# One maximum and one factor operation per attention job: a VectorE reduction over two PSUM banks

## What is computed

```python
# q, k: (B, S, DA_HEADS, 2, 64)   v: (B, S, DA_HEADS, 128)
s = jnp.einsum('bqhcd,bkhcd->bhcqk', q_blk, k).astype(jnp.float32) * scale
...
p = jax.nn.softmax(jnp.where(causal, s, -jnp.inf), axis=-1)
attn = p[:, :, 0] - lam_full * p[:, :, 1]
return jnp.einsum('bhqk,bkhe->bqhe', attn.astype(v.dtype), v)
...
o = o * lax.rsqrt(jnp.mean(o * o, -1, keepdims=True) + RMS_EPS) * subln_g * (1.0 - lambda_init)
```

## Time and profile before

| | us |
|---|---|
| median of 3 runs | 2817.95 |
| lowest and highest | 2817.34 to 2820.68 |
| the profiled execution | 2818.15 |
| its span in the trace | 2815.5 |
| second attention in it | about 959 to 1058 |

### The profile page before, as it was taken

How to read it: one execution, slowest core, us unless ns; L and a number is a source line. 1 busy time by engine, 2 the same in 40 slices (tenths; PEclk the granted TensorE clock), 3 DMA queues, 4 the chain that set the end, 5 groups by cost and what they waited for, 6 DMA issues and landing times. The chain is left out here.

```text
span 2815.5 us, 88317 instructions
## 1 busy us (share of the span) xinstructions
PE 2367.7 (84%) x38648; PEld 1634.8 (58%) x38649; DVE 1051.7 (37%) x2786; ACT 568.3 (20%) x1201; POOL 147.4 (5%) x256
## 2 busy tenths in 40 slices
PE   8987897999889989799867659978887879788982
PEld 3436655777644565577645524458886347566761
DVE  0205634333330283433212145026666643232324
ACT  1113411111230261111100021024341111011111
POOL 0000010000000011000000010011112100000001
PEclk9998999999989999899988879989998799999996
DMA  6120307898442101979999942100001349999995
GB/s 240 64 86 5 135 17 265 354 397 327 167 162 98 60 1 56 401 311 393 428 429 428 428 174 93 60 1 3 3 3 42 121 186 417 429 428 428 404 428 228
DMA packets 83114, 612.46 MB, mean 218 GB/s; under 512 B 19810, under 2 KB 40546, under 8 KB 49188
## 3 DMA queue, kind: packets, MB, share of 16 engines
q1 hardware_dynamic: 44864, 569.05, 48.8%
q10 hardware_dynamic: 31396, 20.06, 2.3%
q0 software_dynamic: 6720, 21.40, 2.3%
HBM read 578.99 MB, written 31.46 MB: 217 GB/s over the span
## 5 line engine op out<-in xcount | busy, mean ns | idle before, releaser
L1175 PE MATMUL ps<-ring,arena 128*32 128x128 f32 x13184 | 408.1, 283 | 102.6 <-DMA ring<-in_experts 72.6
L1175 PEld LDWEIGHTS ps<-ring,arena 128*32 128x32 f32 x13184 | 378.7, 114 | 144.2 <-DMA ring<-in_experts 68.8
L1152 PE MATMUL ps<-x_tok,arena 128*32 128x256 f32 x4768 | 300.5, 392 | 24.5 <-DVE arena L1289 19.7
L1382 DVE TENSOR_TENSOR arena<-arena,ps 128x64 f32<-128x64 f32 x292 | 64.8, 222 | 611.2 <-ACT arena L1234 611.2
L1234 ACT ACTIVATE arena<-ps 128x64 f32<-128x64 f32 x292 | 65.5, 224 | 1089.0 <-PE ps L1175 1089.0
L1152 PEld LDWEIGHTS ps<-x_tok,arena 128*32 128x32 f32 x4768 | 163.2, 114 | 106.2 <-issue 37.9
L1175 PE MATMUL ps<-arena 128*32 128x128 f32 x5504 | 172.9, 285 | 48.5 <-DMA arena<-in_experts 39.9
L1185 PE MATMUL ps<-ring,arena 128*32 128x256 f32 x3296 | 198.7, 379 | 9.4 <-DMA ring<-in_experts 9.4
L1175 PEld LDWEIGHTS ps<-arena 128*32 128x32 f32 x5504 | 159.6, 114 | 67.2 <-DMA arena<-in_experts 45.6
L1126 PE MATMUL ps<-ring,arena 128*128 128x512 f32 x384 | 170.7, 600 | 3.1 <-PEq L192 2.1
L1185 PEld LDWEIGHTS ps<-ring,arena 128*32 128x32 f32 x3296 | 110.2, 110 | 80.0 <-DMA ring<-in_experts 15.2
(11 more groups left out here) (418 smaller groups left out, 3068.5 us busy)
## 6 DMA issues: line engine op xcount, KB each, us to landing
ring<-in_experts SPq DMA_DIRECT2D x165, 2048.0 KB, 21.5
arena<-in_experts SPq DMA_DIRECT2D x50, 2048.0 KB, 24.7
xt_mem<-in_experts SPq DMA_DIRECT2D x25, 2048.0 KB, 29.2
ring<-in_mixer_chunks SPq DMA_DIRECT2D x24, 2048.0 KB, 12.4
xybuf<-arena ACTq DMA_DIRECT2D x608, 32.0 KB, 6.7
xybuf<-arena SPq DMA_DIRECT2D x1, 9216.0 KB, 25.6
rows<-in_ln_g POOLq DMA_DIRECT2D x6, 512.0 KB, 7.4
rows<-in_ln_b POOLq DMA_DIRECT2D x6, 512.0 KB, 8.4
```

Source lines behind the costliest of these rows:

```text
L1152: ins = pe.matmul(ps[to, 5, 0:W], one_hot[:, j, :], x_tok[:, j, q * W:(q + 1) * W], start=(j == 0), stop=(j == NT - 1))
L1175: ins = pe.matmul(ps[at, 2 + half, 0:P], xg[:, k, :], w_gu[half][:, k, q, :], start=(k == 0), stop=(k == NK - 1))
L1382: dve.tensor_tensor(hidden[:, half, :], silu_g[:, half, :], ps[:, 2 + half, HALF:P], ALU.mult)\
```

## The change

For `n_comp == 2` the two maxima of a job are taken by one TENSOR_REDUCE whose input is both banks (128 partitions x 2 x width) and whose output is two columns, and both factors by one TENSOR_SCALAR on two columns. DVE waits once, for both score tiles. The semaphore `dve_a` is counted up once per job instead of twice, and both of ACT's exponentials wait for that one count. The first attention (`n_comp == 1`) takes the same path as before.

```diff
-            m0, x0, e0 = pe_a.take(jobs * n_comp), dve_a.take(jobs * n_comp), act_a.take(jobs * n_comp)
+            m0, x0, e0 = pe_a.take(jobs * n_comp), dve_a.take(jobs), act_a.take(jobs * n_comp)
...
                             for c in range(n_comp):
-                                act.wait_ge(dve_a.sem, x0 + n_comp * s + c + 1)
+                                act.wait_ge(dve_a.sem, x0 + s + 1)
...
+                    def joint_maxima(n):
+                        m = st[:, n % DEEP, :]
+                        dve.wait_ge(pe_a.sem, m0 + 2 * n + 2)
+                        link(dve.tensor_reduce(m[:, 0:2], ps[:, 2 * (n % 2):2 * (n % 2) + 2, 0:width(n)], AX, ALU.max))
+                        dve.tensor_scalar(m[:, 2:4], m[:, 0:2], -SCALE, None, ALU.mult).then_inc(dve_a.sem, 1)
+
                     def maxima(n):
                         m = st[:, n % DEEP, :]
+                        if n_comp == 2:
+                            return joint_maxima(n)
                         for c in range(n_comp):
```

## The result

| | before | after |
|---|---|---|
| median of 20 runs, us | 2819.27 | 2826.46 |
| lowest and highest | 2814.76 to 2824.20 | 2822.44 to 2833.59 |
| profiled execution (its span) | 2818.15 (2815.5) | 2828.93 (2827.2) |
| second attention, first product to last head | 99.04 | 107.29 |
| DVE busy in it | 78.60 | 72.43 |

The ratio is 1.0026, with a 95% interval of 1.0019 to 1.0032. That is 7.2 us more, where +2.2 was forecast, and 2826.46 lies above the range (2825.0). The middle of the interval is over the bound of 0.2%, its lower end just under it; to "slower by over 0.2%" 0.18 had been given. The kernel before was measured 1.3 us above the three runs that the forecast started from; that leaves 5.0 us between the forecast difference and the measured one.

A forecast was written before the change was run, and what follows sets the result against it. A loop of dependences, no engine full, bounds the steady head. Five heads' 2.2, first interval's 0.17 and -0.15 for table load and tail give +2.2 us: 2820.2 us after taking off 0.20, range 2816.0 to 2825.0.

The forecast's parts named there:

- A: Steady head, 512-wide maximum's start to the 256-wide job's product on PE: 3.16 us, forecast +0.32 through ACT's queue.
- Rival 3: Joint reduction over two banks is dear: +1.06 us a head, 2826.6 us in all; chance 0.07.
- rival 1: DVE's whole saving arrives: 8.0 us less, 2810.0 us; chance 0.05.
- the last addend of A: Step from the end of ACT's store to PE's product, taken as 0.05 us from a PE weight load.
- B: Steady head, from the 384-wide job's maxima to the next waiting product on PE: 2.63 us, forecast +0.12.
- PE's stretches: The two parts of a steady head where PE works without pause, 1.80 and 2.67 us, forecast unchanged.
- The head: One steady head of the second attention, 10.26 us between 512-wide maxima, forecast +0.44 in five intervals.
- First interval: Interval from job 3's maxima, with no store to wait for: forecast +0.17 us or so.
- table load: Job 27's head, exponentials behind a table load: up to 0.25 us gained; -0.15 taken with the stage's end.
- tail: End of the second attention: up to 0.25 us gained; -0.15 taken together with the table load.
- rival 4: PE's clock falls to half in longer pauses: +3.9 us in all with one, +5.5 two, +7.2 three; two or more 0.14.
- POOL beside the difference for 512 columns: DVE's line 927 starts about when POOL starts squares; would stay hidden with about 0.1 us left.

The follow-up runs named there:

- both_counts: Kernel before, with only ACT's wait changed: both exponentials of a job wait for the second factor; ratio 1.0029.
- store_first: Kernel after, with ACT's store of job s-4 moved ahead of the exponentials in the second attention, the copy staying behind them; ratio 0.9995.
- before_order: Kernel before, with ACT's copy and store moved ahead of the exponentials and nothing else changed; ratio 1.0001.
- filler: Kernel after, with four useless matrix products on PE ahead of the transposes of each 384-wide job; ratio 1.0023, run again 1.0020.
- one_count: Kernel after, with PE's score semaphore counted up once per job instead of once per score tile; ratio 1.0024.
- csf_two_factors: Kernel after, with ACT's copy and store ahead of the exponentials and the joint factor split into two one-column operations; ratio 0.9999.
- csf_pool_late_one: Kernel after, ACT's copy and store ahead of exponentials, POOL's squares after the next head's difference, one score count per job; ratio 0.9991, again 0.9988.

## Why the prediction was wrong in size and right in kind

- **What bounds the head**: right. It is a loop of dependences, DVE's saving off A does not count, and ACT's queue takes its place. That ACT's later release carries it is shown by both_counts, and that the store's place in the queue matters, by store_first. The sentence that ACT was beside the loop before, only near, was wrong: before_order shows 0.16 a head.
- **What DVE saves**: right. First maximum to reciprocal takes 992.36 - 991.02 = 1.34 (forecast 1.33, before 1.58). The factor takes 0.169 instead of the assumed 0.15; ACT starts 1.47 after the maximum, where 1.44 or 1.45 was forecast. Rival 3 falls with the 1224 ns of the joint reductions, rival 1 with DVE's idle time in the stage, which grew from 20.4 to 34.9 us; the forecast said about 10 more, it was 14.4 in the longer stage.
- **A, forecast +0.32, measured 994.61 - 991.02 = 3.59, so +0.43**: this is the step of the prediction that failed, and it is a size: the last addend of A, from the store's end to PE's product, was taken as 0.05, from a pair in the earlier trace rows that is DVE's difference and PE's weight load. For the store it is 994.61 - 994.46 = 0.15. The rest of the chain, 3.43 by the addends, came to 3.44. The right value stood in the earlier trace rows, read wrongly: the store ended 0.15 before the product at A and 0.15 before it at B, which I took for slack. The same 0.15 after the change says that it was the step from the one to the other, and that ACT's store was the last to come before the change too. Moved by its own 0.43 (its end 3.01 after the maximum before, 3.44 after), it moves the product by 0.43.
- **B, forecast +0.12, measured 2.83 against 2.63, about +0.20**: the store's end moves from 2.48 to 2.69 after the maximum, as much as the product. The forecast moved it from 995.73 to 995.95 too, by 0.22, and then lost 0.10 of that by the same addend. The upper bound of 0.17 rested on it as well.
- **PE's stretches, forecast unchanged, measured +0.05 each**: 1.85 for 1.80 and 2.72 for 2.67. The joint reduction starts 0.073 after the last score product's end, the single one started 0.030 after. I had priced the wait for both tiles at nothing because the second tile was early enough; the wait itself has a price. Half of it goes with one count.
- **The head, forecast +0.44, measured +0.73**: 0.43 + 0.20 + 0.05 + 0.05. In five intervals that makes 3.7 instead of 2.2.
- **First interval, table load, tail**: first +0.50 for the 0.17 forecast, of which B and PE's stretches, if they have the sizes measured in the steady head, make 0.30 and A the remaining 0.20 where 0.07 was forecast; the table load's head -0.13 at full clock (13.05 in filler for 13.18) as forecast; tail +0.10, where a gain was forecast.
- **The clock**: rival 4 happened as it was described, beside the forecast and not in place of it. PE had been busy 1.75 of the 3.40 us before the fall, within the 1.7 to 1.9 that were worked out; the fall cost 1.22 and not 1.66. The second fall, in the table load's head, was not foreseen: PE was busy 0.83 of the 3.40 us before it. A chance of 0.14 for two or more was too low. The prediction called three falls bad luck, but the kernel after had its two in the same heads in both of its profiles, one_count too, and both_counts had two in its steady heads and one in the table load's. The fall in the table load's head does not need longer heads: store_first, csf_two_factors and before_order have it as well. How much of the falls is in the medians stays open, as said.
- **POOL beside the difference for 512 columns**: it happened, DVE at 994.47 and POOL at 994.55. But DVE was first by 0.08, and it was POOL that took 1.58 us for 1.04; the difference took 0.75. No wait for POOL was seen in the steady head.
- **The profile after**: 10.99 is above the 10.8 that was named as the bound at which the prediction is wrong.

Together, the intervals at full clock make 4.1 us of the stage (0.50 + 3.65 - 0.13 + 0.10) where 2.2 was forecast, and the two falls 2.8 in the profile (1.22 and 14.59 - 13.05), for which the forecast had nothing. That is 6.9, near the 7.2 of the medians; but the filling, which has the 4.1 without the falls, is at +6.5 and +5.6 in the runs. So the part of the queue is shown, 1.9 of the 5.0 us by which the forecast difference was too small, and for the rest the falls are the likely cause and not the shown one.

## What to carry to other kernels

Before merging two operations, ask who waits for the first of them, and what is queued behind that waiter; here the merge saved 0.25 us a job on an engine with slack and held four queued operations of the next. It paid only together with an order in which the queue behind it was empty of what others wait for, and in which POOL, beside which the merged factor took 0.86 us, was not set free at that moment. And the step from an operation's end to the start of its waiter is a term of its own, read from the same pair of engines: a gap that comes back at meeting after meeting of the two, 0.15 at A and at B here, before and after, is that step and no slack.

## What the runs showed of the hardware

- From the end of ACT's store to the start of PE's waiting product it was 0.15 us; from the end of DVE's difference to PE's weight load 0.05 to 0.06 (993.48 to 993.54).
- After a wait for two counts DVE's reduction began 0.073 us after the modelled end of the last score product, with one count 0.048, and before, after the wait for the first tile alone, 0.030.
- A TENSOR_SCALAR on 128x2 in SBUF, begun 0.21 us into POOL's TENSOR_TENSOR, ended only 0.03 after it (0.86 for 0.17 us); one on 128x1 was not held so, and neither was a RECIPROCAL on 128x2 (0.16 at 992.00) nor a reduction out of PSUM. In csf_pool_late_one, DVE's reduction and POOL stood so:

```profile
1014.02 1.04 POOL L776 TENSOR_TENSOR xt_mem<-arena 128x512 f32<-128x512 f32 x1 [8.84 <-DVE xt_mem L941]
...
1014.33 0.69 DVE L916 TENSOR_REDUCE small<-ps 128x2 f32<-128x512 f32 x1 [0.44 <-PE ps L794]
```

- DVE's difference for 512 columns and POOL's TENSOR_TENSOR, each with two inputs in SBUF: with DVE 0.06 to 0.08 us ahead, as in six heads of the kernel after, it took its 0.75 and POOL 1.58 for 1.04. At 1054.27 in the same trace DVE was ahead by 0.04, and there it was DVE that took longer, and ended 0.55 after POOL:

```profile
1054.27 1.63 DVE L935 SCALAR_TENSOR_TENSOR xt_mem<-xt_mem,small 128x512 f32<-128x512 f32 x1
1054.31 1.04 POOL L774 TENSOR_TENSOR xt_mem<-arena 128x512 f32<-128x512 f32 x1 [11.77 <-ACT arena L860]
```

- PE's clock fell at 1006.5 although no pause of PE in that head was longer than 1.12 us (1.12 ahead of its transposes, 0.52 ahead of the product); the same head at full clock has PE busy 9.25 of 10.99 us.
